# A two-direction delta-rule scan inside a three-block model: scan slots put in another order

## What is computed

```python
def step(state, inp):                      # state: 64 x 64 per head
    r_t, w_t, k_t, v_t, kk_t, a_t = inp
    sa = einsum('bhvk,bhk->bhv', state, -kk_t)
    state = state * w_t[..., None, :] + sa[..., None] * (kk_t * a_t)[..., None, :] \
            + v_t[..., None] * k_t[..., None, :]
    return state, einsum('bhvk,bhk->bhv', state, r_t)
...
w_log = -softplus(-(w0[d] + tanh(xw @ w1[d]) @ w2[d])) - 0.5
decay = exp(-exp(w_log));  a = sigmoid(a0[d] + (xa @ a1[d]) @ a2[d]);  g = sigmoid(xg @ g1[d]) @ g2[d]
kd = k * (1 + (a - 1) * k_a)
bonus = sum(r * kd * r_k, per head) * v
dir_out = (group_norm(o, gn_w, gn_b) + bonus) * g      # group norm per head: (o - mean) / sqrt(var + eps)
```

## Time and profile before

| | |
|---|---|
| three runs | 2968.63, 2981.57, 2982.03 us; median 2981.57 |
| profiled execution | 2990.23 us, of which the span from first to last instruction 2988.1 |
| busy in the span | TensorE 86%, its weight loads 59%, DVE 43%, ACT 36%, POOL 27% |
| mean granted TensorE clock | 0.942 |
| scan stage | about 1084 to 1900 us of the span |

### The profile page before, as it was taken

How to read it: one execution, slowest core, us unless ns; L and a number is a source line. 1 busy time by engine, 2 the same in 40 slices (tenths; PEclk the granted TensorE clock), 3 DMA queues, 4 the chain that set the end, 5 groups by cost and what they waited for, 6 DMA issues and landing times.

```text
span 2988.1 us, 47159 instructions
## 1 busy us (share of the span) xinstructions
PE 2577.9 (86%) x18708; PEld 1766.0 (59%) x18708; DVE 1285.1 (43%) x2202; ACT 1088.3 (36%) x1959; POOL 819.3 (27%) x469
## 2 busy tenths in 40 slices
PE   4999979999969957777777777779999889999999
PEld 2876648888624436555555555338788566673443
DVE  4036532011281344655555555242941269972302
ACT  3246633233241135544454443123643222235011
POOL 2310144444300033222222221034444433331103
PEclk9999989999989979988989888889999999999999
DMA  2221013232212200000000000113442233322222
GB/s 103 85 66 49 21 48 91 92 99 85 84 37 76 62 6 2 7 7 8 2 8 7 7 2 2 57 37 97 167 131 90 72 97 120 110 88 71 77 78 71
DMA packets 49728, 180.62 MB, mean 60 GB/s; under 512 B 5584, under 2 KB 5712, under 8 KB 49296
## 3 DMA queue, kind: packets, MB, share of 16 engines
q1 hardware_dynamic: 45920, 166.98, 17.8%
q10 hardware_dynamic: 3632, 11.08, 0.9%
HBM read 167.49 MB, written 10.55 MB: 60 GB/s over the span
## 4 chain that ended last, share of the span: by engine, by line
PE 72%; DVE 9%; issue 8%; ACT 8%; POOL 3%; DMA 1%; DVEq 0%; ACTq 0%; POOLq 0%; SPq 0%
PE ps L552 15%; PE ps L548 11%; PE ps L549 11%; PE ps L550 11%; PE ps L726 3%; PE ps L642 2%; PE ps L622 2%; POOL h L1983 2%; PE ps L737 2%; PE ps L571 2%; PE ps L709 2%; PE ps L700 2%; POOL ring_lo L1970 1%; ACT arena L1307 1%; PE ps L716 1%
## 5 line engine op out<-in xcount | busy, mean ns | idle before, releaser
L1970 POOL TENSOR_TENSOR ring_lo<-ring,ring_hi 128x1024 fp32r<-128x1024 f32 x198 | 495.7, 2511 | 736.4 <-ACT ring_hi L1037 736.4
L552 PE MATMUL ps<-arena,ring 128*128 128x512 f32 x1024 | 452.4, 602 | 41.0 <-DVE arena L1682 20.7
L549 PE MATMUL ps<-u_lo,ring_hi 128*128 128x512 f32 x968 | 384.6, 397 | 0.0
L552 PEld LDWEIGHTS ps<-arena,ring 128*128 128x128 f32 x1024 | 196.3, 193 | 296.4 <-issue 275.0
L1037 ACT ACTIVATE ring_hi<-ring 128x1024 fp32r<-128x1024 f32 x198 | 207.1, 1051 | 75.3 <-DMA ring<-in_wall 71.9
L548 PE MATMUL ps<-mlp_u_hi,ring_hi 128*128 128x512 f32 x512 | 203.6, 398 | 20.6 <-DVE u_lo L1495 20.6
L549 PEld LDWEIGHTS ps<-u_lo,ring_hi 128*128 128x128 f32 x968 | 183.8, 190 | 42.1
L548 PE MATMUL ps<-mid_hi,ring_hi 128*128 128x512 f32 x512 | 202.6, 396 | 0.3 <-POOL ring_lo L1970 0.3
L550 PE MATMUL ps<-mlp_u_hi,ring_lo 128*128 128x512 f32 x512 | 202.8, 396 | 0.0
L550 PE MATMUL ps<-mid_hi,ring_lo 128*128 128x512 f32 x512 | 202.5, 396 | 0.0
L549 PE MATMUL ps<-mid_lo,ring_hi 128*128 128x512 f32 x512 | 202.5, 395 | 0.0
(11 more groups left out here) (422 smaller groups left out, 5082.4 us busy)
## 6 DMA issues: line engine op xcount, KB each, us to landing
ring<-in_wall SPq DMA_DIRECT2D x273, 512.0 KB, 3.7
s_tables<-arena ACTq DMA_DIRECT2D x16, 512.0 KB, 3.0
arena<-s_tables SPq DMA_DIRECT2D x16, 512.0 KB, 3.6
arena<-bias_lines SPq DMA_DIRECT2D x16, 448.0 KB, 4.4
arena<-in_lora SPq DMA_DIRECT2D x8, 384.0 KB, 3.1
h<-in_x SPq DMA_DIRECT2D x1, 2048.0 KB, 8.1
out<-arena ACTq DMA_DIRECT2D x8, 256.0 KB, 2.8
consts<-in_consts SPq DMA_DIRECT2D x1, 1378.0 KB, 11.6
```

The lines of the kernel that those rows point to most:

```text
L549: nc.tensor.matmul(y, w_hi, low, start=False, stop=False)
L552: mm = nc.tensor.matmul(bank((t0 + j) % 2), ring[:, at:at + P], rhs(x), start=x == 0, stop=x == k - 1)
L1970: G.tensor_tensor(ring_lo[:, slot], ring[:, slot], ring_hi[:, slot].bitcast(F32), ALU.subtract).then_inc(sem("weights_split"), 1)
```

## The change

The same products, masks and functions are issued in another order, with these differences in what is done:

- `out_mean` and `out_center` are gone: v is turned with `center` (identity minus the mean over the head) instead of `ident`, into O[d] instead of B[d]; the scan's outputs are then centred already. `out_square` reads the outputs from PSUM, right after the first round of the next slot.
- The scaling of the state moves from DVE to ACT (`scan_s` there, Copy with a scale from SBUF).
- The three output products of a chunk and the start of the next w move to a new `scan_o` at the end of each round, behind the turn of the level and any `hidden_out` or output product.
- Mr's scores are made after Mb's in round 1 and masked in round 2; `spread_ro` moves from the end of the slot before to round 0; be is turned and copied in round 2.
- `hidden_out` 0 moves to round 2, 1 to level 1, the Sigmoids to level 1, the decay sums to level 1 and the Exps to level 2, `key_factor` to level 2, `decayed` to level 3, `spread_al` to level 4, `hidden_out` 2 to level 4, `gate_in` behind the last level. On POOL `rates` follows the mask of level 3, `scaled_keys` that of level 5.
- The variance product comes at level 2, the bonus product at level 3 behind the Sqrt, DVE's bonus and first reciprocal at level 4, the second reciprocal behind the last level.

The core of the diff:

```diff
+    put("center", np.eye(P) - heads / HEAD)
...
 # TensorE
-            def out_mean(o, F):
-                pe.wait_ge(sem("o_copied"), unit(o, 1, 1))
-                nc.tensor.matmul(O[o[1]], const("head_mean"), F["al"], start=True, stop=True
-                                 ).then_inc(sem("mean_ready"), 1)
-
             def out_bonus(o, F):
-                pe.wait_ge(sem("o_centered"), unit(o, 1, 1))
+                pe.wait_ge(sem("deviation"), unit(o, 1, 1))
...
             def out_variance(o, F):
-                pe.wait_ge(sem("bonus_done"), unit(o, 1, 1))
...
+                def scan_o(j):
...
+                    if j == 0:
+                        if k:
+                            pe.wait_ge(sem("z_taken"), unit(k, 3, 3))
+                        else:
+                            pe.wait_ge(sem("bonus_done"), unit(o_freed, 1, 1))
+                    pe.nop(nofuse=True)
                     for e in range(2):
-                        mm = nc.tensor.matmul(O[q][e * HEAD:(e + 1) * HEAD, at], u_alone[q][e], R[q]["Mb"][:, at],
-                                              start=False, stop=True)
+                        rows = slice(e * HEAD, (e + 1) * HEAD)
+                        nc.tensor.matmul(O[q][rows, at], v_alone[e][:, at], R[q]["Mr"][:, at], start=True, stop=False)
+                        if j:
+                            nc.tensor.matmul(O[q][rows, at], s_alone[j % 2][q][e], S["ro"][:, at], start=False, stop=False)
+                        mm = nc.tensor.matmul(O[q][rows, at], u_alone[q][e], R[q]["Mb"][:, at], start=False, stop=True)
                     mm.then_inc(sem("o_ready_rw"), 1)
...
                 scan_w(1)
                 if k:
                     pe.wait_ge(sem("n_copied"), unit(k, 1, 1))
                     each_turned(B[d], r["N"]).then_inc(sem("scores_ready"), 1)
+                scan_u(1)
+                if k:
+                    pe.wait_ge(sem("spread"), unit(k, 2, 2))
                     each(A[d], F["be"], r["ro_alone"]).then_inc(sem("scores_ready"), 1)
-                scan_u(1)
-                if f:
-                    pe.wait_ge(sem("masked_v"), unit(k, 3, 1))
-                    hidden_out(f, 0)
                 scan_s(1)
+                if k:
+                    if o:
+                        pe.wait_ge(sem("o_squared"), unit(o, 1, 1))
+                    each(O[d], F["ka"], r["ro_alone"]).then_inc(sem("scores_ready"), 1)
+                scan_o(1)
...
                     if l < LEVELS - 1:
                         level_turn(l)
-                    if o and l == 1:
+                    if f and l == 1:
+                        pe.wait_ge(sem("z_taken"), unit(f, 3, 1))
+                        hidden_out(f, 1)
+                    if o and l == 2:
...
+                        out_variance(o, Q)
+                    if o and l == 3:
                         out_bonus(o, Q)
-                    if o and l == 2:
-                        out_variance(o, Q)
-                    if f and l == 3:
+                    if f and l == 4:
                         if o:
-                            pe.wait_ge(sem("deviation"), unit(o, 1, 1))
+                            pe.wait_ge(sem("bonus_done"), unit(o, 1, 1))
...
                         hidden_out(f, 2)
+                    scan_o(l + 2)
...
-                        each_turned(B[d], v_st).then_inc(sem("scores_ready"), 1)
+                        each_turned(O[d], v_st, "center").then_inc(sem("scores_ready"), 1)
...
 # ACT
+                def scan_s(j):
...
+                    for e in range(2):
+                        ins = nc.scalar.activation(of_head(s_alone[(j + 1) % 2][q][e], e), of_head(bank(4 * q + 2, CH), e),
+                                                   ACT.Copy, scale=of_head(s_ends[q][:, c:c + 1], e))
+                    ins.then_inc(sem("state_ready"), 1)
...
+                scan_s(0)
+                if o:
+                    out_square(o, Q)
+                if k:
+                    spread_ro(k, F)
                 scan_w(1)
...
                 for l in range(1, LEVELS):
                     scan_w(l + 2)
                     if k:
                         level_x(l)
-                        if l < LEVELS - 1:
-                            level_turn(l)
+                    scan_s(l + 2)
+                    if k and l < LEVELS - 1:
+                        level_turn(l)
                     if f and l == 1:
+                        decay_in(f, E)
+                        rate_in(f, E)
+                    if f and l == 2:
                         decays(f, E)
-                    if o and l == 2:
-                        out_square(o, Q)
                     if o and l == 3:
                         out_deviation(o, Q)
-                    if f and l == 3:
+                    if f and l == 4:
                         spread_al(f, E)
-                    if f and l == 4:
-                        gate_in(f, E)
+                if f:
+                    gate_in(f, E)
...
 # DVE
                     if k:
                         level_t(l)
-                    scan_s(l + 2)
                     if k and l < LEVELS - 1:
                         level_pad(l)
-                    if o and l == 2:
+                    if f and l == 1:
+                        decay_sums(f, E)
+                    if f and l == 2:
+                        key_factor(f, E)
+                    if f and l == 3:
+                        decayed(f, E, f_ends)
+                    if o and l == 4:
                         out_bonus(o, Q)
-                    if f and l == 2:
-                        decayed(f, E, f_ends)
-                    if o and l in (3, 4):
-                        out_inverse(o, Q, l - 3)
+                        out_inverse(o, Q, 0)
                 if o:
+                    out_inverse(o, Q, 1)
                     out_scaled(o, Q)
```

More of the change, by code:

```diff
@@ L124 @@
 _at = 0
-for _name, _n in [("mean", P), ("head_sum", P), ("head_mean", P), ("ident", P), ("iota", SEQ), ("carry", SEQ),
+for _name, _n in [("mean", P), ("head_sum", P), ("head_mean", P), ("ident", P), ("center", P), ("iota", SEQ), ("carry", SEQ),
                   ("eye", CH), ("incl", 2 * CH), ("strict", 2 * CH), ("level_n", 2 * CH),
-                  ("level", 2 * LEVELS * CH), ("eps", 4)]:
+                  ("level", 2 * (LEVELS - 1) * CH), ("eps", 4)]:
     CONSTS[_name] = _at
@@ L162, in constants @@
     put("level_n", np.concatenate([both(level(True, 0)), both(level(False, 0))], axis=1))
-    put("level", np.concatenate([both(level(d == 1, l)) for d in range(2) for l in range(LEVELS)], axis=1))
+    put("level", np.concatenate([both(level(d == 1, l)) for d in range(2) for l in range(1, LEVELS)], axis=1))
     put("eps", np.broadcast_to(np.array([NORM_EPS, GN_EPS, 0.0, 1.0], np.float32), (P, 4)))
@@ L701, in each, with each_turned @@
                 return mm
[L703 removed]
+            def each_turned(out, a, by="ident"):
                 pe.nop(nofuse=True)
@@ L708, in each_turned @@
                         rows, at = slice(e * HEAD, (e + 1) * HEAD), slice(c * CH, (c + 1) * CH)
-                        mm = nc.tensor.matmul(out[rows, at], a[:, at], const("ident")[:, e * CH:(e + 1) * CH],
+                        mm = nc.tensor.matmul(out[rows, at], a[:, at], const(by)[:, e * CH:(e + 1) * CH],
                                               start=True, stop=True)
@@ L785, in scan_w @@
                     mm.then_inc(sem("w_ready"), 1)
-                    if j == NCH - 1:
-                        return
-                    for e in range(2):
-                        rows = slice(e * HEAD, (e + 1) * HEAD)
-                        nc.tensor.matmul(C[q][rows, 0:CH], S["ka"][:, at], v_alone[e][:, at], start=True, stop=False)
-                        if j:
-                            nc.tensor.matmul(C[q][rows, 0:CH], const("eye", 0, CH), s_alone[j % 2][q][e],
-                                             start=False, stop=False)
                 def scan_u(j):
@@ L857, in level_t @@
                     pe.wait_ge(sem("tt_taken"), unit(k, 5, l))
+                    if l == 1:
+                        pe.wait_ge(sem("turned"), unit(k, 2, 1))
                     level_product(B[d], r["TT"], r["X_pad"], l, new_columns(d)).then_inc(sem("dt_ready"), 1)
@@ L879, in slot @@
                 scan_s(0)
+                scan_o(0)
                 scan_w(1)
@@ L1376, in _ @@
             spread_al((first, 0), feats[0][0])
-            spread_ro((first, 0), feats[0][0])
             over_pairs(act, pair)
             G = feats[(DT - 1) % 2]
-            slot(None, None, (last, 1), G[1], (last, 0), G[0], None, None)
+            slot(None, None, (last, 1), G[1], (last, 0), G[0], None, None, p_end[(DT - 1) % 2])
             out_square((last, 1), G[1])
@@ L2061, in slot @@
                     level_mask(l)
-                    if f and l == 4:
-                        scaled_keys(f, E)
+                    if f and l == 3:
```

(3 more changed lines are left out.)

144 lines of the change are left out of this document (56 added, 88 removed).

## The result

The changed kernel takes 3011.8 us (median of four runs, 3006.4 to 3027.7) beside 2981.8 us for the kernel before on the same chip: ratio 1.0115, 95% interval 1.0063 to 1.0168. It is slower by 1.15%. The forecast was 2987 us, range 2962 to 3010, with "even" as the most likely case; the time that came lies 1.8 us above the range, next to the third rival's 3009. Of the runs further down one profiled execution, that of experiment 13, took 3165.5 us where its kernel's other four took 2946 to 2953, and isn't used.

The account below looks back on a forecast made before the run. TensorE, with 72% of the chain, was taken to bound the kernel. 14 slots x (+0.7) = +10, with -1.5 and -3.5 at the ends, gave +5 us on 2981.6: 2987 us, range 2962 to 3010.

Parts of the forecast that it names:

- even: Whole kernel: round work gained is paid back in the low clock; 2972 to 2996 us, chance 0.44.
- third rival: Slower: sigmoid wait drops the clock in every slot; three falls, 52.1 us a slot, low time above 18, 3009 us; chance 0.26.
- Mean new slot 46.4, against 47.1: 0.7 us less: Scan stage: mean of backward and forward slots at full clock, 46.4 us new against 47.1 old.
- x to x = 3.9 us, 0.4 less than now: One bare round between level products, scaling off DVE, `scan_o` between turn and w: 3.9 us instead of 4.3.
- The clock term: Each slot: one more clock fall behind the bare sigmoid wait; 15 us low for 10, costing 4.1 us for 2.7.
- -1.5, -3.5: Outside the 14 slots: first two slots and prologue 1.5 us shorter, last slot and tail about 3.5 us shorter.
- x1 at 13.2 (12.8): Backward slot: first level product x1 comes 12.8 us after w0, the slot's first matmul, against 16.0 before.
- the stall of 2.48 (2.6) ahead of `hidden_out` 1: Between level products x1 and x2: TensorE idle 2.6 us, waiting on a sigmoid.
- x3 to x4 above 9: Stretch between level products x3 and x4, with Exp delay and Sqrt wait: 9.25 us, against 7.4 before.
- 0.63 for the scaling (0.62): ACT: scaling the state there takes 0.62 us for the pair, about 0.3 us each.
- u0's copy behind L1765's sum: Forward slots: DVE's output tail ends 3.2 us after w0, holding u0's copy and delaying x1 by 1.5 us.
- no drain at a table load: ACT: table load takes 1.28 us without added drain; rival with a 1.38 us drain gave 3009 us, chance 0.03.

Follow-up runs that it names:

- experiment 13: Changed kernel with the output products back in their old place and the second hidden product moved to level 2, covering the sigmoid: 2950.7 us, ratio 0.9896.
- experiments 2, 9 and 10: Kernel before, in turn: with useless products ahead of its two longest waits, 2953.6 us; with late output products (`scan_o`), 3029.9 us; with both, 2985.4 us.

## Why the prediction went wrong

The stage as profiled and with the stalls filled gives the two parts of each order of outputs:

| | as it is | filled | difference (clock) |
|---|---|---|---|
| kernel before | 697.4 | 660.6 | 36.8 |
| changed kernel | 722.7 | 662.1 | 60.6 |
| changed, outputs back | 673.4 | 635.3 | 38.1 |

These are differences of single profiled executions, and "filled" still holds 7 to 13 us at the low level, some 2 to 4 us of cost, in each. The whole change but the late outputs shortens the stage at full clock by 25.3 us (660.6 to 635.3, 1.8 a slot) and leaves the clock's cost where it was (36.8 to 38.1). The late outputs put 26.8 us of length back (635.3 to 662.1) and 22.5 us of clock on top (38.1 to 60.6). 26.8 + 22.5 - 25.3 + 1.3 = 25.3, the measured growth.

Point by point:

- **The step that failed in the slots: "Mean new slot 46.4, against 47.1: 0.7 us less".** Measured 47.3 against 47.2. The old slot was right; the new one was 0.9 short, a little in each stretch (0.4, 0.2, 0.1, 0.0, 0.2, 0.3 in a backward slot). One part can be read in the rows: w stands right ahead of x, so ACT is still at w's copy when X is ready, and t came at x+1.76 instead of x+1.64; the rest of the 0.9 I haven't traced to its waits. Under it lay an argument: "x to x = 3.9 us, 0.4 less than now" put the outputs where they cost 0.47 a round and never asked what the same round would be without that. The scaling off DVE is what shortens a bare round (4.3 to 3.7 us in the kernel before with it alone); late outputs give part of it back.
- **The clock term was right in size, by luck as to its cause.** Forecast 15 us low for 10 and 4.1 us a slot for 2.7; measured 15.5 us (217 over 14 slots) for 10, and 4.3 for 2.6. But I put its cause in the sigmoid stall alone, and with the outputs back that stall still stands (2.49 us) while the low time is 10 us a slot; with the sigmoid covered and the outputs late it is 6.7 us (2 x 0.07 x 667.2 / 14). In the changed kernel it takes both, the stall and the late outputs. As I read it, which no run shows by itself, late outputs empty the middle of every round beside a stall that already stands there, and then run at the low level behind it, with w and the whole scan behind them. What the two parts win when undone isn't clock alone either: 27 us of the 49 by which the outputs shorten the stage, and some 20 of the 55 of the sigmoid's cover, are length at full clock.
- **The rival "slower: the sigmoid wait drops the clock in every slot" gave the time but not the account.** Its slot of 52.1 us compares with 51.6, its 0.79 in the middle rounds with 0.85 over the stage and 0.83 in a slot of 51.6 us, its bound of 18 us low wasn't reached by the mean slot; and without the shorter slot that the forecast deducted, 15.5 us sufficed.
- **The other step that failed: the ends, "-1.5, -3.5".** The profiled pair shows +7.3 and +4.8, which is 17 us of its miss of 32. 4.1 of it is the first slot, which has the sigmoid stall without output work to shorten it (44.2 us against 40.1; 40.7 when filled). The 3.2 before the first w0 can't be laid on the change: among the kernel before and its versions of experiments 2, 9 and 10, which have the same code up to there, that w0 stands at 1118.7 to 1124.0 us. At the tail the deduction of a mean product and a centring held: from the last u to the last output product it takes 7.1 us instead of 9.1. But the last slot itself went from 27.1 to 32.7 us, at a clock of 0.58 instead of 0.87. In the changed kernel, filled, it takes 32.1 us with late outputs and 28.9 with early ones (at 0.68 and 0.70); in the kernel before, filled, 28.9 with late and 30.4 with early ones. So how much of the tail's loss is the outputs' and how much the clock's isn't shown.
- **Right:** x1 at 13.2 (12.8), the stall of 2.48 (2.6) ahead of `hidden_out` 1, x3 to x4 above 9, 0.63 for the scaling (0.62), u0's copy behind L1765's sum, a stage clock of 0.85 (0.84 to 0.88), no drain at a table load. Turning v with another constant cost nothing that shows, and without the mean product and the centring the program was 14 to 21 us shorter.

By slot: +1.8 us measured (51.6 against 49.8), +0.7 forecast. Of the 1.1 missed, 0.8 is the length at full clock and 0.3 the clock; 14 of them are 15 us, the ends 17 more. Between the medians the miss is 25 us, as the changed kernel's profiled execution lay further above its median than the other.

**What stays open.** Why the changed kernel with the scaling on DVE is 27 to 40 us slower while with early outputs no difference can be told: its low time (18.2 us a slot against 15.5) accounts for 0.8 of the 2.0 us a slot between the stages at 0.28 each, the rest wasn't measured at full clock. And how much of the 50 us of late outputs in the kernel before is length: the fill held the clock only at 0.97 there. The undisturbed slots differ by 1.2 us, backward (47.07 against 45.91) and forward (49.36 against 48.17) alike, some 16 us over 14 slots. Of the 30 us between the two filled stages, another 8 or so are clock by an estimate from their low time (41 against 13 us, at 0.27 each).

## What to carry to other kernels

Independent work behind the last product of a round isn't free because it is short: it belongs in the waits that the round has anyway, and each order has to be priced against the same round without it. Before a stall is moved, look at what else leaves TensorE idle in the same stretch: undoing either of two edits, the sigmoid's place or the outputs', won back 41 us, both together only 61, and each did so partly by a shorter slot and partly by the clock. A filled kernel (useless products ahead of each long wait) is a cheap measurement: it separates a slot's length from what the clock adds, and here it was faster than the kernel it measures. Check that the fill itself adds nothing (an undisturbed slot with it and without it), and compare two filled kernels only where both reach the same clock.

## What the runs showed of the hardware

- Useless matmuls ahead of the stalls made both kernels faster, by 0.8 to 1.0% (before) and 1.6 to 1.9% (changed; by medians and by ratios), with 362 and 546 more matmuls in the stage; the clock rose from 0.90 and 0.85 to 0.99.
- A microsecond at the 1.2 GHz level cost 0.28 us in the changed kernel (60.6 for 217) and 0.26 in the one before (36.8 for 139), less than the 0.45 that a product lost which took 2.07 us instead of 1.13.
- The same stall of 2.5 us behind the sigmoid stood in the changed kernel at 15.5 us of low time a slot and, with the output products back in the middle of the rounds, at 10.
- A scale from SBUF made a 64x64 Copy on ACT 0.09 us dearer, 0.63 against 0.45 for the pair in the changed kernel; the same pair took DVE 0.58.
- The same stall of 2.48 us was followed by a product of 1.13 us at the sigmoid and of 2.07 at the Sqrt of the same slot.
